# Gate and up of a SwiGLU as seven half-size products each (Strassen) in a two-layer decoder kernel on one core

## The reference, cut to what matters

```python
def _rmsnorm(x, g):
    xf = x.astype(jnp.float32)
    xf = xf * lax.rsqrt(jnp.mean(xf * xf, axis=-1, keepdims=True) + EPS)
    return (xf * g.astype(jnp.float32)).astype(x.dtype)

def _swiglu(h, wg, wu, wd):
    return (jax.nn.silu(h @ wg) * (h @ wu)) @ wd
...
# x += 0.5*SwiGLU(RMSNorm(x)), twice in each layer
```

## Time and profile before

| | before |
|---|---|
| median of 3 runs | 2401.24 us (2396.73 to 2401.4) |
| the profiled execution's own time | 2395.91 us |
| its span in the trace | 2394.0 us |
| mean granted TensorE clock | 0.990 of full speed |
| busy: PE, DVE, POOL, ACT | 97%, 43%, 40%, 31% |
| instructions | 49628 |

### The profile page before, as it was taken

How to read it: one execution, slowest core, us unless ns; L and a number is a source line. 1 busy time by engine, 2 the same in 40 slices (tenths; PEclk the granted TensorE clock), 3 DMA queues, 4 the chain that set the end, 5 groups by cost and what they waited for, 6 DMA issues and landing times.

```text
span 2394.0 us, 49628 instructions
## 1 busy us (share of the span) xinstructions
PE 2316.4 (97%) x19159; PEld 2209.4 (92%) x19159; DVE 1041.3 (43%) x1894; ACT 745.0 (31%) x1113; POOL 951.1 (40%) x507
## 2 busy tenths in 40 slices
PE   7999999999998999999999999999999899999998
PEld 7999999889765999999999999988996589999998
DVE  5323324589363432332442332354965614332334
ACT  4222222532453422222242122135225525222223
POOL 3443433356503343343443443433762034344342
PEclk9999999999999999999999999999999999999999
DMA  4433423223677132232322333322328842233231
GB/s 133 122 91 99 106 85 94 59 65 91 211 261 237 54 102 75 89 98 71 111 79 86 105 94 86 96 65 63 82 84 284 269 154 78 73 96 89 77 96 55
DMA packets 333242, 261.38 MB, mean 109 GB/s; under 512 B 35126, under 2 KB 286768, under 8 KB 333104
## 3 DMA queue, kind: packets, MB, share of 16 engines
q1 hardware_dynamic: 330814, 254.60, 36.1%
q0 software_dynamic: 1920, 4.59, 0.5%
q10 hardware_dynamic: 386, 0.52, 0.1%
HBM read 250.86 MB, written 8.85 MB: 108 GB/s over the span
## 4 chain that ended last, share of the span: by engine, by line
PE 91%; SPq 3%; ACT 2%; DVE 1%; DMA 1%; issue 1%; POOL 0%; DVEq 0%; POOLq 0%; ACTq 0%
PE ps L1418 83%; PE ps L1714 2%; SPq L472 1%; PE ps L1815 1%; PE ps L1734 1%; PE ps L1804 1%; SPq L469 1%; PE ps L1796 1%; DMA kp<-in_cache_k 1%; DMA vp<-in_cache_v 1%; PE ps L1578 1%; PE ps L1773 0%; SPq L405 0%; PE ps L1591 0%; DVE rms L1052 0%
## 5 line engine op out<-in xcount | busy, mean ns | idle before, releaser
L882 POOL TENSOR_TENSOR w_lo<-raw,w_hi 128x1024 fp32r<-128x1024 f32 (+1 forms) x336 | 811.1, 2427 | 1313.4 <-ACT w_hi L571 1308.6
L1418 PE MATMUL ps<-h_hi,w_hi 128*128 128x272 f32 x3904 | 803.1, 290 | 23.6 <-POOL w_lo L882 9.4
L1418 PE MATMUL ps<-h_lo,w_hi 128*128 128x272 f32 x3904 | 799.0, 289 | 0.8 <-DVE cat L1317 0.8
L1418 PE MATMUL ps<-h_hi,w_lo 128*128 128x272 f32 x3776 | 784.1, 289 | 0.0
L1418 PEld LDWEIGHTS ps<-h_hi,w_hi 128*128 128x128 f32 x3904 | 612.6, 189 | 32.1 <-issue 25.4
L1418 PEld LDWEIGHTS ps<-h_lo,w_hi 128*128 128x128 f32 x3904 | 613.4, 190 | 2.6 <-issue 2.6
L1418 PEld LDWEIGHTS ps<-h_hi,w_lo 128*128 128x128 f32 x3776 | 592.5, 190 | 0.0
L571 ACT ACTIVATE w_hi<-raw 128x1024 fp32r<-128x1024 f32 (+1 forms) x336 | 340.3, 1038 | 267.4 <-DMA raw<-in_ffn_gate 178.5
L1107 DVE SCALAR_TENSOR_TENSOR xT<-ps,xT 128x544 f32<-128x544 f32 x352 | 250.8, 722 | 175.2 <-PE ps L1418 174.0
L621 ACT ACTIVATE silu<-silu 128x544 f32<-128x544 f32 x88 | 58.0, 660 | 759.0 <-DVE silu L1095 759.0
L1418 PE MATMUL ps<-act_hi,w_lo 128*128 128x272 f32 x1408 | 291.4, 288 | 0.0
(11 more groups left out here) (240 smaller groups left out, 1576.3 us busy)
## 6 DMA issues: line engine op xcount, KB each, us to landing
raw<-in_ffn_gate SPq DMA_DIRECT2D x88, 512.0 KB, 3.8
raw<-in_ffn_up SPq DMA_DIRECT2D x88, 512.0 KB, 3.8
raw<-in_ffn_down SPq DMA_DIRECT2D x88, 512.0 KB, 3.6
kp<-in_cache_k SPq DMA_DIRECT2D x128, 256.0 KB, 3.3
vp<-in_cache_v SPq DMA_DIRECT2D x128, 256.0 KB, 4.8
raw<-in_w_in SPq DMA_DIRECT2D x48, 512.0 KB, 3.7
raw<-in_w_o SPq DMA_DIRECT2D x16, 512.0 KB, 7.4
kipages<-in_cache_kidx SPq DMA_DIRECT2D x128, 32.0 KB, 1.8
```

Of the source, the lines that this page charges most:

```text
L882: pool.tensor_tensor(w_lo[:, c % 6, 0:n], raw[:, c % 3, 0:n], w_hi[:, c % 6, 0:n].bitcast(F32), ALU.subtract).then_inc(units_split, 1)
L1418: ins = pe.matmul(out[:, hf, :], w, x[:, HT * hf:HT * (hf + 1)], start=first and w is w0 and x is xh, stop=last and w is w1)
```

## The change

Gate and up of a block (1024 features x 256 columns, for 544 tokens) are each cut in half in all three directions: features 512 + 512, columns 128 + 128, tokens 272 + 272. By Strassen's scheme in Winograd's form seven products of the halves take the place of eight. A half product is 4 chunks of features x 3 parts = 12 matmuls of 128 x 272 into one bank of PSUM (`half_product`).

- The seven products of gate, and of up, need seven operands of weights, each 128 x 512: three are parts of the raw weights (B11, B21, B22), and four are sums (T1 to T4), which DVE makes in SBUF (`weight_sums`; T1 and T4 in place in the raw slot). For x the operands are two plain parts, the four sums and differences S1, N2, S4 and S3, and A22. DVE makes them once for each instance (`sums_of_x`, `last_differences`), ACT and POOL split them (`high_s`, `low_s`).
- The products' seven sums of each of gate and up are made by DVE in PSUM, in place (`sum_c11`, `sum_u4_c22` and so on) with the first product copied to SBUF by ACT (`p1_out`), and the scaling by `rms` reads them there (`scaled`).
- All weight splits of the SwiGLU have half the size, 128 x 512: 18 for each block (7 + 7 for gate and up, 4 for down), in a ring of nine slots (`ring_hi`, `ring_lo`) that replaces the six slots of 1024. Down of block j waits for all its four halves. There are four raw slots instead of three, two of them shared by gate's weights and down's rows.
- The order of a block in the ring is `LATER` (gate's seven, up's seven, down's four). In an instance's first block it is `FIRST`: the four plain products first, then T4 of both, then gate's other four, then up's. The order of x's chunks in `WO` and in the last down of layer 0 is changed too (`ORD`).

The core of the diff:

```diff
+NRH = 9
...
+FIRST = ['B11g', 'B21g', 'B11u', 'B21u', 'T4g', 'T4u'] + [n + m for m in 'gu' for n in ('T2', 'T1', 'T3', 'B22')]
+LATER = [n + m for m in 'gu' for n in ('B11', 'T2', 'B21', 'T3', 'T1', 'T4', 'B22')] + ['D00', 'D10', 'D01', 'D11']
...
+                def next_gate_up(j):
+                    for r, w, n, done in ((2, up, 0, 27), (3, up, 1, 28), (0, gate, 0, 31), (1, gate, 1, 32)):
+                        hold(sp, "sp", halves_split, fb + done + 18 * j)
+                        load_half(r, column(w, j + 2, n))
...
+
+                hold(pool, "pool", halves_hi, inst * S_FFN + nth)
+                slot = ring_slot(n)
+                pool.tensor_tensor(ring_lo[:, slot, :], half_src(name), ring_hi[:, slot, :].bitcast(F32), ALU.subtract).then_inc(halves_split, 1)
...
-                with pool.Fori(0, FB - 1) as j:
-                    for c in range(4, 10):
-                        lo(l, ph, j, c)
...
+                with pool.Fori(0, FB - 2) as j:
+                    for q in range(8, 26):
+                        lo_half(inst, LATER[q % 18], 14 + q, 15 + q + 18 * j)
...
+            def weight_sums(inst, m, i, kinds):
+
+                low, high = raw4(2 * m), raw4(2 * m + 1)
+                b11, b21, b12, b22 = low[:, 0:512], low[:, 512:1024], high[:, 0:512], high[:, 512:1024]
+                for kind in kinds:
+                    if kind == 'T3':
+                        dve.wait_ge(f_loaded[2 * m + 1], ffn_loads(inst, 2 * m + 1, 'B', i))
+                        dve.tensor_tensor(t3[m][:, :], b22, b12, ALU.subtract).then_inc(t_done[m], 1)
...
+                        dve.tensor_tensor(b12, b12, b11, ALU.subtract).then_inc(t_done[m], 1)
+                    elif kind == 'T2':
+                        dve.wait_ge(t_done[m], t_count(inst, i, 'T1'))
...
+                        dve.tensor_tensor(b11, b21, t2[m][:, :], ALU.add).then_inc(t_done[m], 1)
...
+                def sum_c11(m, bank, tile, p1):
+
+                    dve.wait_ge(tiles, tile)
+                    dve.wait_ge(p1_read, s0 + p1)
+                    dve.tensor_tensor(ps[:, bank, 0:HT], ps[:, bank, 0:HT], p1s[:, m, :], ALU.add).then_inc(sums, 1)
...
+                def gate_times_up(i, m):
+                    dve.wait_ge(silu_done, s0 + 2 * i + 2)
+                    dve.wait_ge(up_done, s0 + 2 * i + 2)
+                    dve.tensor_tensor(gated[:, m, :], gated[:, m, :], silu[:, m, :], ALU.mult).then_inc(gu_done, 1)
...
+                def block(j, buf, last=False):
+                    i, tj, si = j + 1, t0 + 14 + 22 * j, sb + 14 + 14 * j
+                    weight_sums(inst, 1, i, ABC)
+                    sum_u2(0, 5, tj + 2, 3 + 2 * j)
+                    gate_times_up(j, 0)
+                    sum_c11(0, 6, tj + 3, 3 + 2 * j)
+                    gate_times_up(j, 1)
+                    sum_u3(0, 0, tj + 4, si + 2)
+                    weight_sums(inst, 1, i, ('T4',))
+                    sum_u4_c22(0, 3, tj + 5, si + 3)
+                    sum_c21(0, 2, tj + 6, si + 3)
+                    sum_c12(0, 7, tj + 7, si + 4)
+                    dve.wait_ge(gu_done, s0 + 2 + 2 * j)
+                    scaled(0, 6, 0, si + 7)
+                    scaled(0, 2, 1, si + 6)
+                    sum_u2(1, 5, tj + 9, 4 + 2 * j)
+                    act_low(j, buf, 0)
+                    sum_c11(1, 0, tj + 10, 4 + 2 * j)
+                    act_low(j, buf, 1)
+                    sum_u3(1, 6, tj + 11, si + 9)
+                    sum_u4_c22(1, 3, tj + 12, si + 10)
+                    sum_c21(1, 2, tj + 13, si + 10)
+                    sum_c12(1, 1, tj + 14, si + 11)
+                    dve.wait_ge(act_ready, s0 + 2 + 2 * j)
+                    scaled(1, 0, 0, si + 14)
+                    scaled(1, 2, 1, si + 13)
                     for c in range(KC):
-                        add_chunk(j, t0 + 12 * j + 9, c)
-
-                with dve.Fori(0, (FB - 1) // 2) as jj:
-                    step(2 * jj, 1)
-                    step(2 * jj + 1, 0)
-
-                for c in range(KC):
-                    add_chunk(FB - 1, t0 + T_FFN - 7, c)
-                    if nxt[1] == 0 and nxt[0] < DEPTH and c % 2:
-                        low_x(*nxt, c - 1)
-                    if c >= 2:
-                        add_square(norm_no(*nxt), c - 1)
-                add_square(norm_no(*nxt), KC - 1)
+                        add_chunk(j, tj + 15, c, c)
+                        if last and c in (0, 1):
+                            gate_times_up(FB - 1, c)
+                        if last and c in (3, 4):
+                            act_low(FB - 1, 0, c - 3)
+                        if c == 3 and not last:
+                            weight_sums(inst, 0, j + 2, ABC)
+                        if c == 4 and not last:
+                            weight_sums(inst, 0, j + 2, ('T4',))
...
+            def half_product(name, bank, slot, ks):
+
+                for k in ks:
+                    xh, xl = a_chunk(OPERAND[name[:-1]], k)
+                    wh, wl = (w[:, slot, P * k:P * (k + 1)] for w in (ring_hi, ring_lo))
+                    for n, (w, x) in enumerate(((wh, xh), (wh, xl), (wl, xh))):
+                        ins = pe.matmul(ps[:, bank, 0:HT], w, x, start=k == 0 and n == 0, stop=k == 3 and n == 2)
+                return ins
...
+                def product_of(q, j):
+
+                    halves_ready(inst, 15 + q + 18 * j)
+                    if q in (0, 2, 3, 4):
+                        pe.wait_ge(x_updates, xb - 3 + (0, 0, 1, 2, 3)[q] + 8 * j)
+                    if q == 0:
+                        pe.wait_ge(gr_done, s0 + 2 + 2 * j)
+                    elif q == 3:
+                        pe.wait_ge(up_done, s0 + 2 + 2 * j)
+                    elif q == 7:
+                        pe.wait_ge(p1_read, s0 + 3 + 2 * j)
+                    elif q in (8, 9):
+                        pe.wait_ge(sums, sb + (15, 17)[q - 8] + 14 * j)
+                    elif q in (10, 11):
+                        pe.wait_ge(gr_done, s0 + q - 7 + 2 * j)
+                    half_product(LATER[q], LATER_BANK[q], ring_slot(14 + q), range(4)).then_inc(tiles, 1)
+
+                def down(i, j, first_slot, buf, order, last=False, turn=2):
+
+                    halves_ready(inst, S_FFN if last else 32 + 18 * j)
                     pe.wait_ge(act_ready, s0 + 2 * i + 2)
                     for c in range(KC):
-                        p = c % 4
-                        if c >= 4 or i is FB - 1:
+                        p, oc = (c + turn) % 4, order[c]
+                        if c >= 4:
                             pe.wait_ge(x_updates, xb + 8 * i + c - 3)
+                        elif last:
+                            pe.wait_ge(x_updates, xb + 8 * i - 8 + ((7, 8, 8, 8), None, (5, 6, 7, 8))[turn][c])
                         else:
-                            pe.wait_ge(gr_done if p < 2 else up_done, s0 + 2 * i + 3 + p % 2)
+                            if c == 0:
+                                pe.wait_ge(p1_read, s0 + 2 * i + 4)
+                            if c < 2:
+                                pe.wait_ge(sums, sb + 14 * i + (22, 24)[c])
+                            else:
+                                pe.wait_ge(up_done, s0 + 2 * i + c + 1)
                         for m in range(2):
-                            wh, wl = (w[:, (c0 + m) % 6, c * P:(c + 1) * P] for w in (w_hi, w_lo))
+                            cols = slice(P * (oc % 4), P * (oc % 4) + P)
+                            wh, wl = (w[:, ring_slot(first_slot + 2 * (oc // 4) + m), cols] for w in (ring_hi, ring_lo))
                             ins = product(pair(p), wh, wl, act_hi[:, buf, m, :], act_lo[:, buf, m, :], m == 0, m == 1)
                         ins.then_inc(tiles, 1)
...
+                def block(j, buf):
+                    for q in range(14):
+                        product_of(q, j)
+                    down(j, j, 14 + 14, buf, range(KC))
```

More of the change, by code:

```diff
@@ new lines, in ffn, with column, gate_up, down_row @@
+                fb = inst * S_FFN
+                def column(w, i, n):
+                    return w[l, :, :, ds(i * 256 + P * n, P)]
+                def gate_up(i, waits):
+                    for r, w, n, done in ((0, gate, 0, 0), (2, up, 0, 2), (1, gate, 1, 1), (3, up, 1, 3)):
+                        hold(sp, "sp", halves_split, fb + waits[done])
+                        load_half(r, column(w, i, n))
+                def down_row(i, m):
+                    load_half(m, down[l, ds(i * 256 + m * P, P), :], k_first=False)
@@ L626, in act_high, with p1_out, half @@
                         act.activation(act_hi[:, buf, m, :], gated[:, m, :], ACT.Copy).then_inc(acthi_done, 1)
-                root(norm_no(l, ph), 3)
-                hi(l, ph, 0, 3)
+                def p1_out(m, bank, tile, free=None):
+                    act.wait_ge(tiles, tile)
+                    if free is not None:
+                        act.wait_ge(sums, free)
```

(45 more changed lines are left out.)

649 lines of the change are left out of this document (466 added, 183 removed).

## The result

The changed kernel takes 2473.23 us, median of four runs (2469.84 to 2474.94), against 2401.32 of the kernel before: a ratio of 1.0302, with an interval of 1.0284 to 1.032. It is 3% slower, by 72 us. Forecast were 2434 us, 33 more than before; the time lies inside the stated range, but the change is over twice the one forecast. The profiled execution has a span of 2473.1 us against 2394.0, with a mean granted clock of 0.958 against 0.990.

A forecast was written before the change was run, and what follows sets the result against it. TensorE bounds the kernel before; in the changed loop POOL, held up by DVE, sets the pace. 2395.9 - 25 (loops) + 24 + 24.5 + 10 (openings) + 5 (clock) = 2434 us; range 2320 to 2502.

The forecast's parts named there:

- TensorE's own time: In each block, 264 matmuls at 0.1253 us take 33.08 us, 3.01 less than before.
- the rival of one bank for twelve matmuls in a row: Half products: matmuls into one bank run slower; at 25 ns each +72 us, 2506; chance 0.04.
- POOL and DVE shut each other out: Each DVE operation with two SBUF inputs beside a busy POOL costs POOL 0.45 us; nine a block, 4.05.
- The chain of a block: Loop: 35.46 us from down to down, TensorE waiting 2.4 ahead of each; 40 periods give -25 us.
- neither rival of a weaker shutting out: POOL beside DVE: no shutting out for halves, 2290 to 2310, chance 0.13; half of it, 2310 to 2380, chance 0.10.
- The openings: Before each instance's loop, DVE's sums and waits cost +24 us (instance 0), +24.5 (2), +5 each (1 and 3).
- the +5 for the clock: Openings of instances 0 and 2: longer TensorE waits lower the granted clock, +5 us (0 to +10).
- The clock in the loops: Loop: the wait of 2.4 us ahead of each down was given no clock cost.
- a rival with a chance of 0.10: Loop: the wait halves the clock over down's first chunks, every other block: 20 x 3.4 = +68 us, 2502; chance 0.10.

The follow-up runs named there:

- experiment 3: Changed kernel with six more small DVE additions a block in 36 of 40 blocks: 2482.47 us with SBUF inputs, 2473.31 us with one input from PSUM.
- experiment 1: Changed kernel with each loop block's last half product made twice, 12 matmuls more, filling most of the wait ahead of down: 2446.47 us.
- experiment 4: Kernel before, with one wait added: down of a block waits for ACT's high parts of the next block's activations: 2547.18 us.
- experiment 2: Changed kernel with down's first four chunks waiting for two weight halves, the last four for the other two, except in last downs: 2371.44 us.

## Why the prediction was wrong, step by step

- **TensorE's own time.** Right. A block's 168 matmuls of half products take 21.1 us, 0.1254 each, so the rival of one bank for twelve matmuls in a row has no place.
- **POOL and DVE shut each other out.** Right, with a subtraction at 1.73 beside weight sums, 0.48 more against the 0.45 taken. Experiment 3 shows that it is the SBUF inputs, not the length of DVE's queue; for smaller operations elsewhere in the block 0.18 was left of it. One reading was loose, and no term rests on it: the 1.9 each of rows 6 is a mean of three operations that stood beside POOL, 2.5 to 3.0, and two behind it, 0.77.
- **The chain of a block.** Right: 35.34 against 35.46, with a wait of 2.11 against 2.4, released by POOL as forecast. Without the clock the loops gave -28.9; -25 was forecast. So neither rival of a weaker shutting out came about.
- **The openings.** Right in size: +23.2 for +24, +25.5 for +24.5, +7.6 and +6.3 for +5 each; with the +5 for the clock 63.5 were forecast and 62.6 came. In instance 2 the wait of 5.0 for the seven additions of squares, behind DVE's last low parts, was named; the 5.9 for POOL's low parts of the sums was not. That the total came within 1 us is in part luck: the time at half the clock went from 10.2 to 34.1 us in the opening of instance 0 and from 0 to 20.5 in that of instance 2. An estimate: 106 matmuls more begin at half the clock in the two, 0.10 longer each, at most 10.7 us where the sum had 5; DVE's and POOL's part was then smaller than forecast.
- **The clock in the loops: the step that failed.** The forecast put the loops' clock at no cost with a wait of 2.4 in every block, because a single shorter wait, of 1.75, kept it, and left a fall to a rival with a chance of 0.10. Experiments 1 and 4 show that such a wait alone brings the clock down. That rival is what came, in another size: 24 of 40 downs at 1.52, +36.5, where it had 20 at 3.4, +68. The rival's 3.4 was half of the 6.82 us stretch of rows 8; a stretch in a down lasts 3.41 us, half as long, and costs 1.52. With 36.5 for this term, the sum is 2470.5.
- **The mixing parts** had no term and cost 8.6. From the last down to the next first down, with the openings behind, their time at half the clock went from 34.1 to 68.3 us. What shifted it wasn't tried.

## What to carry to other kernels

A wait of TensorE that recurs in every block is priced twice: as idle time, and as the slower clock behind it, if nothing in the trace of before shows a wait of that length which left the clock alone. Look then at what the wait is really for: here a wait for four buffers where two would do, with the slower clock behind it, cost 102 us (experiment 2) of the 132 that TensorE was to be spared, and three lines made the change 1.2% faster than before instead of 3% slower. Work for a narrow path (DVE beside POOL) belongs where TensorE has other work to do: plain products in the first block cost 96 matmuls more, 12 us, and the kernel still gained 39.

## What the hardware showed that was not expected

- A single wait of TensorE of 2.11 (changed kernel) or 2.57 us (experiment 4) once in a block of 35 to 39 us was followed by 3.41 us at 1.2 GHz in 24 and 27 of 40 blocks, and by 2.4 GHz throughout in the others. One of 2.24 (experiment 3) was in four of four. Waits of 0.62 to 1.09 (experiment 1), and two of about 1.5 in one block (experiment 3), were not. Why it is two blocks in three, and not all, stays open.
- TensorE with 12 matmuls more a block was faster by 27 us, since they kept its clock.
